# Merging the high and low token halves into one 512-column matmul in the feed-forward projections of a two-block network

## The reference, cut to what matters

```python
D_MODEL = 1024
D_FF = -(-8 * D_MODEL // (3 * 256)) * 256      # 2816
# h = rms_norm(x, g_ffn): [256 tokens, 1024]
# gate, up = h @ w_gate_up, each [256, 2816]
# x = x + (silu(gate) * up) @ w_down
```

## Time and profile before

| | us |
|---|---|
| median of 3 runs | 2482.31 (2481.39 to 2483.24) |
| span of the profiled execution | 2481.9 |
| PE busy | 2326.2 (94%), 16176 matmuls |
| PE's loads of stationary operands busy | 2102.3 (85%) |
| DVE busy | 1336.7 (54%) |
| ACT busy | 1029.2 (41%) |
| POOL busy | 249.5 (10%) |
| mean granted TensorE clock | 0.972 of 2.4 GHz |

### The profile page before, as it was taken

The page is one execution under the profiler, slowest core; times in us unless marked ns, Lnnn a source line. Parts: engine busy times, 40 slices in busy tenths (PEclk is TensorE's granted clock), DMA queues, the critical chain, the costliest instruction groups (busy, mean ns, idle before and its releaser), DMA issues.

```text
span 2481.9 us, 38412 instructions
## 1 busy us (share of the span) xinstructions
PE 2326.2 (94%) x16176; PEld 2102.3 (85%) x16176; DVE 1336.7 (54%) x2731; ACT 1029.2 (41%) x1963; POOL 249.5 (10%) x252
## 2 busy tenths in 40 slices
PE   5999999999999999899999899998888999988998
PEld 3888878988868988789999899998778999867998
DVE  5544424567643223555556764366756555666554
ACT  2434312454432233444434453453644444554443
POOL 0100001312101121000022311200100110100110
PEclk7999999999999999999999999999989999989999
DMA  6321143211234122232242224363232544312543
GB/s 244 112 70 69 51 170 136 72 67 69 71 117 153 69 85 86 77 119 104 102 152 103 81 90 151 132 202 131 84 119 104 186 173 167 134 51 103 187 167 139
DMA packets 50412, 291.45 MB, mean 117 GB/s; under 512 B 8960, under 2 KB 13312, under 8 KB 19072
## 3 DMA queue, kind: packets, MB, share of 16 engines
q1 hardware_dynamic: 50240, 289.00, 32.5%
HBM read 286.89 MB, written 2.36 MB: 117 GB/s over the span
## 4 chain that ended last, share of the span: by engine, by line
PE 77%; DVE 15%; ACT 5%; issue 2%; POOL 0%; DMA 0%; DVEq 0%; SPq 0%; ACTq 0%; POOLq 0%
PE PS L506 75%; DVE wl L1916 3%; PE PS L510 2%; DVE wl L1918 2%; ACT TM L1345 2%; ACT wh L1355 2%; ACT TMG L1345 2%; DVE TM L1897 1%; DVE colS L1905 1%; DVE HYl L1905 1%; DVE TM L1905 1%; DVE colS L2382 1%; DVE TMG L1905 1%; DVE colS L2217 1%; DVE colS L1901 0%
## 5 line engine op out<-in xcount | busy, mean ns | idle before, releaser
L506 PE MATMUL PS<-HYh,wh 128*128 128x256 f32 (+1 forms) x3000 | 952.4, 317 | 35.4 <-DVE HYl L1905 14.8
L506 PE MATMUL PS<-HYl,wh 128*128 128x256 f32 (+1 forms) x3000 | 937.4, 312 | 0.0
L506 PE MATMUL PS<-HYh,wl 128*128 128x256 f32 (+1 forms) x3000 | 937.1, 312 | 0.0
L1916 DVE TENSOR_TENSOR wl<-raw,wh 128x1280 fp32r<-128x1280 f32 (+2 forms) x254 | 372.1, 1465 | 535.4 <-ACT wh L1355 535.1
L506 PEld LDWEIGHTS PS<-HYh,wh 128*128 128x128 f32 x3000 | 579.2, 193 | 78.3 <-DVE HYl L1905 17.2
L506 PEld LDWEIGHTS PS<-HYh,wl 128*128 128x128 f32 x3000 | 578.7, 193 | 30.3
L506 PEld LDWEIGHTS PS<-HYl,wh 128*128 128x128 f32 x3000 | 579.7, 193 | 28.8
L1355 ACT ACTIVATE wh<-raw 128x1280 fp32r<-128x1280 f32 (+2 forms) x254 | 306.8, 1208 | 342.1 <-PE PS L506 269.0
L506 PE MATMUL PS<-wh,HYh 128*128 128x256 f32 x1458 | 426.2, 292 | 20.4 <-DVE HYl L1905 11.2
L506 PE MATMUL PS<-wl,HYh 128*128 128x256 f32 x1458 | 416.8, 286 | 0.0
L506 PE MATMUL PS<-wh,HYl 128*128 128x256 f32 x1458 | 416.7, 286 | 0.0
(11 more groups left out here) (180 smaller groups left out, 1774.9 us busy)
## 6 DMA issues: line engine op xcount, KB each, us to landing
raw<-in_wpk SPq DMA_DIRECT2D x235, 1024.0 KB, 4.8
raw<-in_wpk SPq DMA_DIRECT2D x32, 704.0 KB, 4.0
TM<-in_wpk SPq DMA_DIRECT2D x4, 1024.0 KB, 17.4
X<-in_xin SPq DMA_DIRECT2D x1, 2048.0 KB, 9.0
Y<-in_wpk SPq DMA_DIRECT2D x2, 1024.0 KB, 23.7
Y<-bias_d SPq DMA_DIRECT2D x4, 512.0 KB, 9.9
raw<-in_wpk SPq DMA_DIRECT2D x3, 512.0 KB, 3.7
T<-in_tabs SPq DMA_DIRECT2D x1, 1216.0 KB, 15.9
```

What stands on the lines that cost most here:

```text
L506: return P.x.matmul(o, l, r, start=start, stop=stop)
L1916: D.x.tensor_tensor(wl[:, s, 0:c], raw[:, r, 0:c], wh[:, s, 0:c], ALU.subtract).then_inc(*lo_split.mark())
```

## The change

The two tiles of activations become one, `HY`, with the low parts 8192 columns behind the high ones, and `hy` gives a third view that runs over both. Gate, up and down products are made with two matmuls in place of three: the weights' high part by 512 columns (high tokens, then low tokens) into both halves of a bank, and the weights' low part by the 256 high tokens into the first half. The result is the sum of the halves. A gate/up unit thus takes two banks (three pairs in turn), ACT copies the second halves to SBUF (`lows`), DVE adds them to the first halves ("gu_sum") and then scales in SBUF ("gu_in"). For down, DVE adds both halves to X2, one after the other. In ACT's queue silu and mid, and in DVE's the product, come one iteration later.

```diff
-        HYh = sb("HYh", [128, 8192], F32R)
-        HYl = sb("HYl", [128, 8192], F32R)
+        HY = sb("HY", [128, 2, 8192], F32R)
...
-        def gu_bank(j):
-            return (j + 2) % 4
+        def gu_banks(j):
+            b = (2, 4, 0)[j % 3]
+            return PS[:, b:b + 2]
+
+        def dn_bank(j):
+            return (0, 2)[j % 2]
+
+        low_sums = [tm(1536 * i, [2, 256]) for i in range(2)]
...
+            def proj_halves(o, u, c0, hl, ready, k0, kn, *events, start=True, stop=True):
+
+                w, v = weights(u)
+                for k in range(kn):
+                    P.wait_ge(*ready(k0 + k))
+                    mm(o, w[:, k, c0:c0 + 128], hl[2][:, :, k0 + k], start and k == 0, False)
+                    t = mm(o[:, 0:256], v[:, k, c0:c0 + 128], hl[0][:, k0 + k], False, stop and k == kn - 1)
                 t.then_inc(*projected.mark(*events))
...
                 for j in range(22):
                     u = place["gu", 22 * l + j]
-                    if j >= 4:
-                        P.wait_ge(dve_step, ("gu_in", l, j - 4))
-                    elif j < 2:
-                        P.wait_ge(act_step, (("x", l), "exp", j))
-                    else:
-                        P.wait_ge(dve_step, (("x", l), "x", j))
-                    two(u, gu_bank(j), GB, normed(f"gffn{l}"), ("gu", l, j))
+                    if j >= 3:
+                        P.wait_ge(dve_step, ("gu_sum", l, j - 3))
+                    elif j == 2:
+                        P.wait_ge(dve_step, (("x", l), "x", 3))
+                    for c in range(2):
+                        if j == 0:
+                            P.wait_ge(act_step, (("x", l), "exp", c))
+                        elif j == 1:
+                            P.wait_ge(act_step, (("x", l), "wt", 2 + c))
+                        proj_halves(gu_banks(j)[:, c], u, 128 * c, GB, normed(f"gffn{l}"), 0, 8, ("gu", l, j), *([("unit", u)] if c else []))
...
-                            P.wait_ge(dve_step, ("dn", l, j - 2) if j >= 2 else ("gu_in", l, 18 + j))
-                        proj_t(bank(j % 2)[:, 0:256], u, 0, 128, MID, lambda k: (pool_step, ("mid", l, k)), 11 * i, 11, 0, 256,
-                               ("dn", l, j, i), ("unit", u), start=i == 0, stop=i == 1)
+                            P.wait_ge(dve_step, ("dn", l, j - 2) if j >= 2 else ("gu_sum", l, 21 if j else 20))
+                        proj_halves(bank(dn_bank(j)), u, 0, MID, lambda k: (pool_step, ("mid", l, k)), 11 * i, 11,
+                                    ("dn", l, j, i), ("unit", u), start=i == 0, stop=i == 1)
...
+                def lows(j):
+                    A.wait_ge(projected, ("gu", l, j))
+                    if j >= 2:
+                        A.wait_ge(dve_step, ("gu_sum", l, j - 2))
+                    act(low_sums[j % 2], gu_banks(j)[:, :, 256:512], ACT.Copy, ("gu_low", l, j))
+
                 for j in range(22):
                     used("gu", 22 * l + j)
                     if j == 1:
                         norm_copy(f"gffn{l}")
-                        silu(l, 0)
+                    lows(j)
                     if j:
-                        silu(l, j)
-                        mid(j - 1)
+                        silu(l, j - 1)
+                    if j >= 2:
+                        mid(j - 2)
+                silu(l, 21)
+                mid(20)
                 mid(21)
...
                 def scaled(j):
-                    D.wait_ge(projected, ("gu", l, j))
-                    D.wait_ge(act_step, ("rs", f"gffn{l}"))
+                    D.wait_ge(act_step, ("gu_low", l, j))
                     if j >= 4:
                         D.wait_ge(pool_step, ("mid", l, j - 4))
-                    tt(g_of(j), v2(gu_bank(j)), rs2x2, ALU.mult, ("gu_in", l, j))
+                    tt(g_of(j), gu_banks(j)[:, :, 0:256], low_sums[j % 2], ALU.add, ("gu_sum", l, j))
+                    D.wait_ge(act_step, ("rs", f"gffn{l}"))
+                    D.wait_own(dve_step)
+                    tt(g_of(j), g_of(j), rs2x2, ALU.mult, ("gu_in", l, j))
...
-                    if j:
-                        product(j - 1)
+                    if j >= 2:
+                        product(j - 2)
+                product(20)
                 product(21)
...
-                    tt(X2[:, j], bank(j % 2)[:, 0:256], X2[:, j], ALU.add, ("dn", l, j))
+                    for c in range(2):
+                        if c:
+                            D.wait_own(dve_step)
+                        tt(X2[:, j], bank(dn_bank(j))[:, 256 * c:256 * c + 256], X2[:, j], ALU.add, ("dn", l, j))
```

More of the change, by code:

```diff
@@ L288, in hy @@
         def hy(base, kn, n):
-            return (HYh[:, base:base + kn * n].rearrange("p (k t) -> p k t", k=kn),
-                    HYl[:, base:base + kn * n].rearrange("p (k t) -> p k t", k=kn))
+            parts = HY[:, :, base:base + kn * n].rearrange("p s (k t) -> p s k t", k=kn)
+            return parts[:, 0], parts[:, 1], parts
         Yf = Y[:].rearrange("p k t -> p (k t)")
@@ L528, in proj_t @@
                             hl[1][:, k0 + k, t0:t0 + n], start and k == 0, stop and k == kn - 1)
+                t.then_inc(*projected.mark(*events))
+            def proj_halves(o, u, c0, hl, ready, k0, kn, *events, start=True, stop=True):
[4 more added lines that the diff above has]
+                    t = mm(o[:, 0:256], v[:, k, c0:c0 + 128], hl[0][:, k0 + k], False, stop and k == kn - 1)
                 t.then_inc(*projected.mark(*events))
```

## The result

| | before | after |
|---|---|---|
| median | 2482.77 (2481.39 to 2484.95, 4 runs) | 2526.64 (2524.17 to 2529.25, 4 runs) |
| ratio, 95% interval | | 1.0173 (1.016 to 1.0187) |
| span of the profiled execution | 2481.9 | 2522.4 |
| matmuls | 16176 | 15120 |
| PE busy | 2326.2 (94%) | 2326.1 (92%) |

Slower by 44 us, where 1056 matmuls are gone. The forecast was 2525 in a range of 2510 to 2540. An execution takes 1.8 us more than its span. The profile of the changed kernel is that of its quickest run (2524.17), so the two profiles lie 40.5 us apart where the medians lie 43.9 apart.

A forecast was written before the change was run, and what follows sets the result against it. PE issue bounded the kernel before; after, ACT and DVE waiting for each other would bound gate/up. Two layers of +21.25 us give +42.5 on 2482.3, so 2525 us, range 2510 to 2540.

The forecast's parts named there:

- The ring: Gate/up: ACT and DVE wait for each other through their in-order queues, period 6.96 us a unit, not 5.76; chance 0.78.
- The rival of a clock that falls with the gaps: Gate/up: PE's idle gaps also lower its clock towards 1.2 GHz, giving 2530 to 2559 us; chance 0.12.
- The sum: Per layer: +21.6 gate/up, -0.6 first units, -0.2 to the end of down, +0.45 last add; +21.25, two layers +42.5 us.
- PE's waits ahead of down units 1 and 2: Start of down: unit 1 waits for weights till 10.8 us, unit 2 for its convert till 15.5.
- the queue of SP: not late: Gate/up: raw weight loads land in 4.8 us and are wanted 7.6 us later, so cost nothing.
- The last add: End of each layer's down: the second add is in the open, +0.45 us.
- PE's gain: Gate/up and down: 13.3 ns saved per removed matmul, 14.1 us for 1056 if PE stayed the bound everywhere.
- the wide matmul's price: 512-column matmul reading two pieces 32 KB apart: extra cost between nothing and 13.3 ns, taken as nothing.
- Had PE been the bound: Rival for gate/up: ACT and DVE don't hold PE back, -14.1 + 0.9 gives 2469 us; chance 0.07.
- 2.5 ns per matmul: Skill's fixed cost beside the columns; down's gain would be 0.9 us instead of 4.7; set aside for the trace.
- The half-way rival: Gate/up: only the two weight buffers bind, 5.9 us a unit, total 2482 us; chance 0.03.

The follow-up runs named there:

- Run 3: The changed kernel with three matmuls of 256 columns again; banks, copy, sum and queues as changed: 2531.34 us, ratio to before 1.0195.
- run 1: The changed kernel with DVE's weight convert and product queued ahead of its sum and scaling: 2481.27 us, ratio to before 0.9989.
- run 2: The changed kernel with ACT's copy of the low halves queued ahead of its weight convert: 2480.36 us, ratio to before 0.9985.
- run 4: The changed kernel with ACT's mid one more iteration later (j-3 in place of j-2): 2511.41 us, ratio to before 1.0114.
- run 6: The changed kernel with ACT's copy first, silu, product and mid at their old lag, and high and low tokens side by side: 2479.12 us, ratio 0.9982.

## Why the prediction was right

**The ring.** Forecast 6.96 us a unit, measured 6.89. The steps of one unit add up to it in the rows: 1.16 + 0.74 to the copy (forecast 1.92 together), 0.61 to the sum (0.63), 0.72 to the scaling (0.73), 0.61 to wl, 1.40 + 0.87 to the product (1.41 + 0.87), 0.45 and 0.33. Run 3 shows that PE has no part in it, runs 1 and 2 that either queue's order opens it, run 4 that mid's wait for the product closes it. The rival of a clock that falls with the gaps is out: the granted clock was 0.99 and 1.00 in the two stages, though PE idles 1.2 to 1.3 us in each unit (6.89 less 5.55 to 5.65). The Trainium skill's account of micro-idles that make the clock oscillate (TensorE: Matmul & The Clock Gate, A second HAM failure mode) isn't borne out at gaps of this length.

**The sum.** From the convert of j = 0 to that of j = 20 the working gives 21.6 - 0.6 = +21.0 us a layer, measured +20.0, mostly by the 0.07 us that the period is shorter. From the convert of j = 20 to PE's last matmul of down it gives -0.2. Measured there are 69.1 us before and 69.2 after in the first layer, 69.0 and 69.8 in the second: +0.1 and +0.8. PE's waits ahead of down units 1 and 2 came as forecast: they start 10.7 and 15.6 us after that convert, 10.8 and 15.5 were worked out. What was left out are some 0.08 us at the first matmul after each stall in both layers, and in the second a further wait. There "the queue of SP: not late" failed. The chain of waits in the second layer has a load in it (start, us, what):

```profile
2454.22 0.96 DVE wl L1943
2455.18 0.75 DVE wl L1945
2455.95 5.56 DMA raw<-in_wpk
2461.53 0.86 ACT wh L1373
2462.41 0.96 DVE wl L1943
```

At the start of down the converts come late, a raw buffer comes free late with them, and the load of a later unit took 5.56 us from there, where the median of such loads of 704 KB is 4.0. I had looked at the load in the ring's steady state alone. Its unhidden part is small, a step of 0.46 us in place of 0.12 ahead of the matmul at 2464.25. Why this load took longer than others isn't shown. The last add cost as forecast: two adds in 0.88 us where there was one of 0.42.

The parts of the sum err both ways: gate/up was 2 us less than forecast in all, the ends of the stages 1.3 more, and the rest of the program 1.3 less. How near the number came is in part luck; that it lies in the range isn't.

**PE's gain.** 13.3 ns per removed matmul holds at the better of two paces, 6.7 ns at the other. The bounds given for the wide matmul's price (0 to 13.3 ns) hold both paces. The value taken, nothing, was true of one pace only, and the reason given for a price (two pieces) was wrong, as run 6 shows. Had PE been the bound, 14.1 us would have been 7 to 14. That is one part of what is missing in run 1. Its profile lies 12 us above the forecast: 3.4 of them are the slower pace in gate/up (114.3 us for 112.6, twice), 3.6 lie in down (61.3 and 61.0 us, where 61.2 - 2.35 + 0.5 = 59.4 was expected), at the start of which its converts come late, and 3.6 lie outside of both stages. The 2.5 ns per matmul that the prediction cites from the Trainium skill (TensorE: Matmul & The Clock Gate, Back-to-back issue gap) is what that section gives for an isolated matmul and not for a stream; for the streams here the rows decide, 13.3 ns.

**The half-way rival** (two weight buffers alone, 5.9 us) was mis-sized: run 4 has 6.43, since PE's unit counts 5.98 from its start to ACT's convert and the scaling that met POOL's subtraction took 0.53 longer.

## What to carry to other kernels

An added step is priced by what stands behind it in its queue, not by its length alone: here a copy of 0.6 us on an engine 47% busy, with the sum that waits for it, cost some 45 us, since it linked the heads of two in-order queues into a ring, and swapping two lines in either queue took the cost away. When an edit makes an instruction wait for another engine, add up the ring through both queues, start to start, before its merit on the bound engine. And a gain per instruction that is read off a uniform stream should be measured in the mixed stream that will run.

## What the runs showed that I had not expected

- A stream in which matmuls of 512 and 256 columns alternate runs at one of two paces, 346.7 or 353.4 ns a pair, set anew by a stall and kept after it. Long streams of one width have one pace here (120.0 and 227.4 ns). Grouping like matmuls removed the choice (5.59 us a unit in all units, against 5.55 or 5.65).
- A DVE instruction of 0.69 us with two SBUF inputs took 1.22 us when it began 0.07 us after a POOL subtraction of 0.74, and 0.69 when it began after its end.
- After most stalls the first 512-column matmul had 302 to 317 ns to the next one, not some 233 (in the changed kernel from 2350.36 to 2350.67), some 75 ns once per stall.
- Behind the first layer's down the granted clock falls in other places from profile to profile, and the time outside of the two stages went from 2125.4 to 2131.6 us.
